# A hybrid decoder trunk on one core: all four chunks of the expert down weights in high and low parts

## What is computed

```python
gates = jnp.sum(jax.nn.one_hot(eidx, N_EXPERTS, dtype=jnp.float32) * w[..., None], axis=-2)
out = jnp.zeros_like(t)
for e in range(N_EXPERTS):
    hid = jax.nn.silu(t @ w_gate[e]) * (t @ w_up[e])
    out = out + gates[:, e:e + 1] * (hid @ w_down[e])
```

## Time and profile before

| | us |
|---|---|
| median of 3 runs | 1557.18 |
| lowest, highest run | 1555.33, 1567.28 |
| profiled execution | 1552.4 |
| its span in the trace | 1550.9 |

### The profile page before, as it was taken

How to read it: one execution, slowest core, us unless ns; L and a number is a source line. 1 busy time by engine, 2 the same in 40 slices (tenths; PEclk the granted TensorE clock), 3 DMA queues, 4 the chain that set the end, 5 groups by cost and what they waited for, 6 DMA issues and landing times. The chain is left out here.

```text
span 1550.9 us, 17391 instructions
## 1 busy us (share of the span) xinstructions
PE 1356.8 (87%) x6415; PEld 1060.1 (68%) x6415; DVE 1108.3 (71%) x1316; ACT 718.6 (46%) x983; POOL 199.1 (13%) x280
## 2 busy tenths in 40 slices
PE   5399988886989999999919998888698999999991
PEld 2277775565787777777717777656487777777771
DVE  2559875665478888888655987666646888888873
ACT  1233433454137666666413343244513666666650
POOL 0000113600110010000030010252001010001002
PEclk9599998687999999999959999878799999999996
DMA  9355752331278999999654575243208799999945
GB/s 361 118 190 191 235 192 98 122 109 68 77 290 321 406 404 401 400 399 393 223 172 153 177 258 180 96 162 94 84 28 326 261 401 401 394 400 407 406 175 190
DMA packets 95167, 378.52 MB, mean 244 GB/s; under 512 B 5929, under 2 KB 8727, under 8 KB 85736
## 3 DMA queue, kind: packets, MB, share of 16 engines
q1 hardware_dynamic: 71496, 307.78, 52.5%
q0 software_dynamic: 15264, 55.63, 9.3%
q10 hardware_dynamic: 8320, 13.96, 2.6%
HBM read 344.53 MB, written 32.82 MB: 243 GB/s over the span
## 5 line engine op out<-in xcount | busy, mean ns | idle before, releaser
L1098 PE MATMUL ps<-mod_rounded,work_rounded 128*128 128x512 f32 x340 | 138.2, 406 | 1.1 <-DVE work_rounded L1981 1.1
L1100 PE MATMUL ps<-mod_rounded,work_rounded 128*128 128x512 f32 x340 | 133.8, 394 | 0.0
L1847 DVE TENSOR_TENSOR ring_rounded<-ring,mod_rounded 128x2048 fp32r<-128x2048 f32 (+1 forms) x54 | 103.0, 1931 | 23.5 <-ACT mod_rounded L1393 23.5
L1847 DVE TENSOR_TENSOR work_rounded<-work,mod_rounded 128x2048 fp32r<-128x2048 f32 (+1 forms) x48 | 91.4, 1932 | 31.8 <-ACT mod_rounded L1393 31.8
L1099 PE MATMUL ps<-ring_rounded,work_rounded 128*128 128x512 f32 x288 | 113.2, 393 | 0.0
L1489 DVE SCALAR_TENSOR_TENSOR gain<-ring,csil,gain 128x512 f32<-128x512 f32 x134 | 101.8, 760 | 3.0
L1099 PE MATMUL ps<-work_rounded 128*128 128x512 f32 x256 | 100.6, 393 | 0.0
L853 PE MATMUL ps<-ring_rounded,actT_rounded 128*128 128x512 f32 (+1 forms) x256 | 95.7, 374 | 0.0
L1393 ACT ACTIVATE mod_rounded<-ring 128x2048 fp32r<-128x2048 f32 (+1 forms) x54 | 86.2, 1630 | 0.0
L853 PE MATMUL ps<-work_rounded,mod_rounded 128*128 128x512 f32 (+1 forms) x192 | 79.0, 412 | 6.9 <-ACT work L1207 4.0
L1098 PE MATMUL ps<-actT_rounded,work_rounded 128*128 128x512 f32 x204 | 81.0, 397 | 0.0
(11 more groups left out here) (348 smaller groups left out, 3543.7 us busy)
## 6 DMA issues: line engine op xcount, KB each, us to landing
ring<-in_ada_w SPq DMA_DIRECT2D x38, 1024.0 KB, 5.3
ring<-in_moe_w_gate SPq DMA_DIRECT2D x18, 2048.0 KB, 10.1
ring<-in_moe_w_up SPq DMA_DIRECT2D x18, 2048.0 KB, 10.7
ring<-in_moe_w_down SPq DMA_DIRECT2D x18, 2048.0 KB
work<-in_moe_w_gate SPq DMA_DIRECT2D x16, 2048.0 KB, 10.4
work<-in_moe_w_up SPq DMA_DIRECT2D x16, 2048.0 KB, 11.2
work<-in_moe_w_down SPq DMA_DIRECT2D x16, 2048.0 KB, 11.7
expert_rows<-work POOLq DMA_DIRECT2D x34, 512.0 KB, 8.3
```

What stands on the lines that cost most here:

```text
L1098: pe.matmul(ps[j][:, :], xl, hi, start=k == 0, stop=False)
L1100: mm = pe.matmul(ps[j][:, :], xh, hi, start=False, stop=k == KD - 1)
L1847: v.tensor_tensor(slots_r[3 * odd + j][:, 512 * k0:512 * k1], slots[3 * odd + j][:, 512 * k0:512 * k1], buf.bitcast(F32), ALU.subtract).th ...
```

## The change

Chunk 3 of the down weights is treated like the other three. ScalarE rounds it into the first 1024 columns of `actT` (for the last expert into the next 1024), VectorE subtracts, `hT_r` and `hT_lo` hold four pieces instead of three, and TensorE runs 24 fp32r matmuls for each down projection. `h_out` is one copy instead of two. TensorE waits for the three parts one after another inside the first half, where it waited for both parts before the first matmul. `d_hi` and `d_lo` count three parts for each expert. Since `actT` is reused, the combine weights `w12` and `wsum` move to the tile `sml`, and ScalarE waits, for the first expert alone, until the router's tables are done with (`pos_dn`).

```diff
@@ -214,10 +214,9 @@
     chosen = view(0, 2 * T, D)
     square = view(17408, D)
     x_scaled = gain[:]
-    hT_r = view(18432, 3, P, of=work_r)
-    hT_lo = view(19968, 3, P, of=work_r)
+    hT_r = view(18432, 4, P, of=work_r)
+    hT_lo = view(19968, 4, P, of=work_r)
     hT = view(18432, 4, P)
-    hT3 = view(18432 + 384, P)
     xeT_r = view(14336, KD, P, of=work_r)
     xeL = view(18944, KD, P, of=work_r)
     slots_r = [ring_r[:, n, :] for n in range(3)] + [view(4096 * n, 4096, of=work_r) for n in range(3)]
@@ -227,9 +226,10 @@
 
 
 
-    DOWN_SPLIT = 3
-    down_hi_parts = [(0, 2, biasm_r[:, :, :].rearrange("p a b -> p (a b)")), (2, 3, gain_r[:, :])]
-    down_hi_last = [(0, 2, mod_r[:, 2048:4096]), (2, 3, mod_r[:, 4096:5120])]
+    down_hi_parts = [(0, 2, biasm_r[:, :, :].rearrange("p a b -> p (a b)")), (2, 3, gain_r[:, :]),
+                     (3, 4, actT_r[:, 0:2, :].rearrange("p a b -> p (a b)"))]
+    down_hi_last = [(0, 2, mod_r[:, 2048:4096]), (2, 3, mod_r[:, 4096:5120]),
+                    (3, 4, actT_r[:, 2:4, :].rearrange("p a b -> p (a b)"))]
 
     def down_high(e):
         return down_hi_last if e == NTL - 1 else down_hi_parts
@@ -272,8 +272,8 @@
     lose_flat = route[:, 448:704].rearrange("p (q n) -> p q n", q=T * 4)
     lose_g = route[:, 704:768].rearrange("p (q i j) -> p q i j", q=T, i=4)
     lose_g_flat = route[:, 704:768].rearrange("p (q n) -> p q n", q=T)
-    w12 = route[:, 896:904].rearrange("p (a t) -> p a t", a=2)
-    wsum = route[:, 904:908]
+    w12 = sv(824, 8).rearrange("p (a t) -> p a t", a=2)
+    wsum = sv(832, 4)
     j8, j1, r8, ec, base8, rf, tf, pf, t1, ctf = (
         route[:, n:n + 8] for n in (432, 440, 912, 920, 928, 936, 944, 952, 960, 968))
     row_oh = view(18432, 2 * T, P, of=work_r)
@@ -1113,19 +1113,18 @@
                     if not first:
                         pe.wait_ge(y_ev, 2 * e)
                     pe.wait_ge(*expert_loaded(e, odd, 2))
-                    pe.wait_ge(d_lo, 2 * e + 2)
-                    w = slots[n].rearrange("p (k n) -> p k n", k=4)
                     lo_ = slots_r[n].rearrange("p (k n) -> p k n", k=4)
                     for b in range(2):
                         cols = slice(512 * b, 512 * b + 512)
-                        pe.matmul(ps[6 + b][:, :], hT3, w[:, 3, cols], start=True, stop=False)
-                        for k0, k1, buf in down_high(e):
+                        for m, (k0, k1, buf) in enumerate(down_high(e)):
+                            if b == 0:
+                                pe.wait_ge(d_lo, 3 * e + (m + 1))
                             hi_ = buf.rearrange("p (k n) -> p k n", k=k1 - k0)
                             for k in range(k0, k1):
-                                pe.matmul(ps[6 + b][:, :], hT_lo[:, k, :], hi_[:, k - k0, cols], start=False, stop=False)
+                                pe.matmul(ps[6 + b][:, :], hT_lo[:, k, :], hi_[:, k - k0, cols], start=k == 0, stop=False)
                                 pe.matmul(ps[6 + b][:, :], hT_r[:, k, :], lo_[:, k, cols], start=False, stop=False)
                                 mm = pe.matmul(ps[6 + b][:, :], hT_r[:, k, :], hi_[:, k - k0, cols],
-                                               start=False, stop=k == DOWN_SPLIT - 1)
+                                               start=False, stop=k == 3)
                         mm.then_inc(y_ps, 1)
 
                 keep_warm(20)
@@ -1421,8 +1420,7 @@
 
                 def h_out(e):
                     a.wait_ge(ht_ps, e + 1)
-                    a.activation(hT_r, ps[4][:, 0:384].rearrange("p (k n) -> p k n", k=3), ACT.Copy)
-                    a.activation(hT3, ps[4][:, 384:512], ACT.Copy).then_inc(ht_ev, 1)
+                    a.activation(hT_r, ps[4][:, :].rearrange("p (k n) -> p k n", k=4), ACT.Copy).then_inc(ht_ev, 1)
 
                 def down_hi(e, odd):
                     a.wait_ge(*expert_loaded(e, odd, 2))
@@ -1430,7 +1428,9 @@
                         a.wait_ge(gu_ps, 2 * NTL)
                     elif e:
                         a.wait_ge(y_ps, 2 * e)
-                    for k0, k1, buf in down_high(e):
+                    for m, (k0, k1, buf) in enumerate(down_high(e)):
+                        if e == 0 and m == 2:
+                            a.wait_ge(pos_dn, 2)
                         a.activation(buf, slots[3 * odd + 2][:, 1024 * k0:1024 * k1], ACT.Copy).then_inc(d_hi, 1)
 
                 def expert_turn(e, odd, first=False):
@@ -1991,12 +1991,12 @@
 
                 def hidden_low(e):
                     v.wait_ge(ht_ev, e + 1)
-                    v.tensor_tensor(hT_lo, ps[4][:, 0:384].rearrange("p (k n) -> p k n", k=3), hT_r.bitcast(F32),
+                    v.tensor_tensor(hT_lo, ps[4][:, :].rearrange("p (k n) -> p k n", k=4), hT_r.bitcast(F32),
                                     ALU.subtract).then_inc(hl_lo, 1)
 
                 def down_lo(e, odd):
                     for m, (k0, k1, buf) in enumerate(down_high(e)):
-                        v.wait_ge(d_hi, 2 * e + (m + 1))
+                        v.wait_ge(d_hi, 3 * e + (m + 1))
                         cols = slice(1024 * k0, 1024 * k1)
                         v.tensor_tensor(slots_r[3 * odd + 2][:, cols], slots[3 * odd + 2][:, cols], buf.bitcast(F32),
                                         ALU.subtract).then_inc(d_lo, 1)
```

## The result

The changed kernel took 1543.03 us as the median of four runs (1540.73 to 1544.18), the kernel before 1558.13 beside it: a ratio of 0.9891, with a 95% interval of 0.9848 to 0.9934, which is 10 to 24 us. (The ratios here are taken over all runs and differ a little from the quotient of the medians, 0.9903 in this case.) Measured twice more, in e1 and e9, it was 0.9917 (0.9892 to 0.9941) and 0.9933 (0.9906 to 0.9959), so the gain is clear of the noise each time, and about 1%. The medians differ by 15.1, 13.9 and 10.7 us; the forecast had been 6.5.

The account below looks back on a forecast made before the run. TensorE was taken to set the turn, with transfers following. Per layer 15 x 0.25 = 3.75 us saved less 0.48 in the tail gives 3.27, 6.5 for two layers: 1545.9 profiled, median 1550.7, range 1543 to 1560.

Parts of the forecast that it names:

- the three waits: TensorE's waits for parts 1, 2 and 3 in a down's first half: already met, so costed at nothing.
- 24 x 0.230 + 0.09 = 5.61: Down projection: 24 fp32r steps of 0.230 us, plus 0.09 because the first follows fp32 transposes; 5.61 instead of 5.86.
- the price of a turn: Saving on TensorE per down projection: 0.25 us, making the turn 18.11 instead of 18.36 us.
- The prediction's own bound without the 0.09: Upper bound of the saving in a down projection, leaving out the added 0.09: 0.34 us.
- Gate and up were taken as untouched: The gate and up pace, 46 steps at 0.233 us, served only as a bound for the down: 5.69, saving 0.17.
- The delay: Last expert of each layer: VectorE's third subtraction makes TensorE start the last down at 770.50 instead of 769.68, 0.82 later.
- a time outside the loops that moves: Sign of being wrong: any time outside the expert loops that moves, or TensorE waiting in the steady turns.
- a fixed offset of 4.8 us: Whole execution: the profiled run lay 4.8 us below the median 1557.2, so predicted 1545.9 became a median of 1550.7.
- Rival 1 (DMA): Transfers set the pace: turns save nothing, tails cost 2 x 0.48 us, median 1558.2; chance 0.10.
- Rival 2 (VectorE): VectorE becomes the pace in every turn above 1.43 us of added work; with 2.0, median 1569 us; chance 0.08.
- Rival 3 (waits): Three waits in a down at 0.09 us each, with the changed step, eat the gain: median 1558.8; chance 0.09.
- rival 4: fp32r passes in a down run at the fp32 rate, 0.215 us each: a down saves 0.61, median 1539.1; chance 0.05.

Follow-up runs that it names:

- e1: The changed kernel again, against the kernel before on the same chip: 1542.62 against 1556.51 us, ratio 0.9917.
- e9: The changed kernel once more, on another chip beside e10: 1544.94 us, ratio 0.9933 to the kernel before.
- e2: TensorE's instructions of the kernel before, with the changed kernel's third rounding on ScalarE and third subtraction on VectorE: 1557.6 us, ratio 1.000 to the kernel before.
- e7: On top of e3, 20 instead of 24 matmuls a down, output wrong: 1513.96 us, ratio 0.9732 to the kernel before.
- e4: The changed kernel with one wait for all three parts before a down's first matmul, instead of three: 1540.46 us, ratio 0.9891 to the kernel before.
- e5: The kernel before with chunk 3's fp32 matmul moved from the head to the end of each half: 1553.67 us, ratio 0.9997 to the kernel before.
- e12: The changed kernel with 11 small matmuls ahead of the wait before the last down: 1540.63 us, ratio 0.9901 to the kernel before.
- e3: The changed kernel's 24 fp32r matmuls, but only two parts on ScalarE and VectorE, output not the layer's: 1539.96 us, ratio 0.9892 to the kernel before.
- e6: The changed kernel with the last expert's third subtraction moved behind the two outputs and the hidden low part: 1540.35 us, ratio 0.9915 to the kernel before.
- e8: The changed kernel with two more 128x512 VectorE multiplications in every turn but the last two: 1548.87 us, ratio 0.9968 to the kernel before.
- e10: The changed kernel with e6's VectorE order, run beside e9 on one chip: 1538.97 us, ratio 0.9882 to the kernel before.
- e11: The changed kernel with 20 small matmuls ahead of the wait before the last down: 1545.31 us, ratio 0.9928 to the kernel before.

## Why the prediction was right and wrong

**The mechanism was right.** TensorE set the turn, VectorE's and ScalarE's new work lay in their waits (e2), the DMA followed (e7), the three waits cost nothing (e4), and VectorE's order in the last expert gave time back. The median lay at the very edge of the range, which the terms of the sum alone did not reach (they ended at 1547.8), and the gain was 2.3 times the forecast in the first measurement and 1.6 times in the last. Of the 8.6 us between forecast and the first difference of medians, the loops hold 1.9: the turns gave 5.2 more than forecast and the tails took 3.3 more. The other 6.7 lie outside the loops.

**The down projection.** Forecast 24 x 0.230 + 0.09 = 5.61, measured 5.62. The rival with passes at the fp32 rate is excluded: the fp32r matmul steps 0.231. Taken with the half of 2.93 us before, the fp32 matmul had cost 2.93 - 9 x 0.231 = 0.85, 0.213 for each of four passes. The Trainium skill, "FP8 and Floating Point Precision", section "TensorE Precision Notes", counts four passes for true fp32, and this case's rows fit that: 0.85 us is four times 0.213. The rule of 216 ns for a warm matmul, cited in the prediction from the Trainium skill, "TensorE: Matmul & The Clock Gate", section "Back-to-back issue gap", and given there for a single matmul by itself, fits those passes; the fp32r matmuls, each with a weight load of its own, step 0.231.

**The step that failed is the price of a turn: 0.25, measured 0.43.** It is a term mis-sized twice.
- "So I add 0.09" counted the change of type at the head of the down, and it is there: 614.67 to 614.99 is 0.32. But the transposes ahead became 0.09 shorter, 0.79 for 0.88. Before, the same cost stood between the transposes and the fp32 matmul. I charged the new edge and did not credit the old one: 0.09 a turn, 3 us in all. The prediction's own bound without the 0.09, 0.34, is what the down and the transposes gave together, 0.33.
- Gate and up were taken as untouched, and lost 0.10, 11.27 to 11.17. The two paces stood in the earlier trace rows, 0.233 and 0.230, and I used them as bounds for the down instead of asking why one kind of matmul has two. e2 and e5 show that it hangs on the place of the fp32 matmul, at the head of a half or at its end. 27 turns of the two layers have it: 2.7 us in all.

Sixteen turns at 0.25 would have been 4.0 a layer; they were 6.55.

**The tail was mis-sized too, the other way.** The delay was right: forecast 770.50 against 769.68, 0.82 later, and from the end of gate and up to the last down's start it is 8.67 us after and 7.84 before, 0.83. Left out was what the longer wait does to the clock: 1.56 us a layer (e12). For the stretch behind the last hidden transposes that makes +2.40 instead of the +0.73 that my terms give.

**The two faults partly cancel.** By my steps 3.3 us a layer were to go; the traces show 4.15 and 4.26. That the forecast of 6.5 for the loops came as near as it did to 8.4 is in part luck.

**What the loops don't explain.** The medians differ by 10.7 to 15.1 us, the loops by 8.4. The prediction named a time outside the loops that moves as a sign of being wrong. The spans of the changed kernel's profiles are 1542.2, 1538.3 and 1538.9, those of kernels with an fp32 matmul in each half 1550.9, 1551.7 (e2) and 1552.3 (e5). The stretch from the end of the first loop's last matmul to the second layer's first steady turn is 443.6 before and 441.1, 440.6 and 438.1 after (e9 the last), but 440.8 in e2 and 443.9 in e5. I find no part of the change in it, and it moves by 3 us within both kinds. Medians less loops leave 0.4 to 7.7 us of gain in e3, e4, e6, e8, e10, e11 and e12 too, 2.2 in e2, but -0.2 in e5 and -2.5 in e7; whether the 2 to 7 us that are left are chance or an effect of the change stays open. That I took the one median as a fixed offset of 4.8 us over the profile was a weak point of the forecast.

**The rivals.** Rival 1 (DMA) fell with e7, where the turn went to 17.02. Rival 2 (VectorE) did not occur, but its threshold was near: 1.1 us more made it the pace in e8. It was not at the 1.43 us of added work that the prediction names: the change added 1.17 (155.70 us of 180 busy before, 171.12 after, over 520 to 700 us) and left 0.88, so the edge is near 2.05. Rival 3 (waits) fell with e4, rival 4 with the steps of 0.231.

## What to carry to other kernels

When an operation is replaced, price both edges of it, the one that appears and the one that vanishes, and read the same kind of instruction in all places of the turn: two paces for one kind are a question, not a bound. Where an engine's new work falls on the path only at the end of a loop, order the last iteration by what the waiting engine needs first; that took 2.65 us a layer off the timeline here. And a wait on TensorE can have two prices, itself and the clock behind it: between 1.46 and 2.54 us, 1.08 us more of waiting cost 2.65 (e10 against e9). When times are this close, a median of a few runs on another chip can hide such a gain, as in e6; the timeline shows it.

## What was not expected of the hardware

- In the last expert TensorE idle for 2.54 us was followed by steps at half the clock (1.2 GHz) in both layers of the changed kernel and of e1, e4, e8 and e9; idle for 1.39 or 1.46 it never was. In between it varies: 2.08 us in e2 brought slow steps in one layer and not in the other, 2.32 us in e7 in neither. With small matmuls in the gap the clock stayed at 1.00. The price was 1.56 us. The length of the gap alone does not decide it: at the start of each loop TensorE idles 1.2 us before the hidden transposes and 0.54 behind them, and in the first layer of e5, e10 and e11 eight steps at 0.43 followed, 1.6 us, elsewhere none.
- The same 48 fp32r matmuls took 11.27 us in a steady turn where an fp32 matmul headed each half of the down, and 11.17 where it stood last or was absent. In the kernel before, the first three turns of the first layer and the first two of the second still had 11.17 to 11.21, though an fp32 matmul headed the halves of the down before the second of them; later ones had 11.27. The cause is open.
- 16 DMA engines at a busy share of 1.00 and 402 GB/s still gave 412 and then 422 GB/s when the loop got faster. A share of 1.00 did not mean that they were the limit; the landing times, flat or growing, told it.
